# Prefix rows staged ahead, and the conv and merge stages of a hybrid retention block ordered by token blocks

## The reference

```python
mod = silu(c) @ w_ada + b_ada                     # six vectors of 1024 for each sequence
sh1, sc1, g1, sh2, sc2, g2 = split(mod)
u = rmsnorm(h) * (1 + sc1) + sh1
q, k, v, og, cb, cc, cx, ga, gb = split(u @ w_in) # 512, 512, then 1024 each
ret = groupnorm(retention(rotary(q), rotary(k), v))       # chunks of 64, carried state
y_ret = (silu(og) * ret) @ w_ret_out
y_conv = (cb * causal_conv3(cc * cx)) @ w_conv_out
h = h + g1 * ((sigmoid(ga) * y_ret + sigmoid(gb) * y_conv) @ w_o)
u2 = rmsnorm(h) * (1 + sc2) + sh2
h = h + g2 * (square(relu(u2 @ w_ff1)) @ w_ff2)
return rmsnorm(h)
```

## Time and profile before

| | us |
|---|---|
| median of 3 runs | 1334.42 (1331.57 to 1335.6) |
| the profiled execution | 1338.04 |
| its span, slowest core (core 2) | 1336.5 |
| spans of the eight cores | 1327.3 to 1336.5 |
| TensorE busy | 1231.7 |
| mean granted TensorE clock, share of full speed, by core | 0.966 to 0.974 |

### The profile page before, as it was taken

One profiled execution on the slowest core, in us unless ns is written; L12 is line 12 of the kernel. 1 busy time (PEld: TensorE's weight loads), 2 busy tenths in 40 slices (PEclk: granted clock), 3 DMA queues, 4 the chain that ended last, 5 costly groups with the idle time before them and its releaser, 6 DMA issues.

```text
span 1336.5 us, 18932 instructions; the slowest of 8 cores (1327.3 to 1336.5 us)
## 1 busy us (share of the span) xinstructions
PE 1231.7 (92%) x6288; PEld 582.0 (44%) x6288; DVE 489.3 (37%) x917; ACT 420.8 (31%) x714; POOL 488.4 (37%) x503
## 2 busy tenths in 40 slices
PE   2467799999999999998999999599999999999997
PEld 0233354444444455554444444254444444444443
DVE  5345366666312277776013234340000351000145
ACT  1354143222211167777321112243330023331011
POOL 1055310000000178886643361046660126663012
PEclk9688899999999999999999999799999999999999
DMA  9769170240713400000958819887545549954323
GB/s 169 181 159 210 50 96 1 38 58 1 91 28 41 69 11 1 1 2 8 144 91 128 151 19 243 200 206 105 80 67 92 95 157 155 139 86 70 65 87 126
DMA packets 86591, 124.33 MB, mean 93 GB/s; under 512 B 4704, under 2 KB 69216, under 8 KB 86496
## 3 DMA queue, kind: packets, MB, share of 16 engines
q0 software_dynamic: 67632, 70.26, 38.5%
q1 hardware_dynamic: 16560, 44.48, 10.5%
q10 hardware_dynamic: 2304, 8.39, 1.6%
HBM read 176.59 MB, written 16.78 MB: 145 GB/s over the span
## 4 chain that ended last, share of the span: by engine, by line
PE 85%; DMA 6%; DVE 3%; POOL 2%; issue 1%; another core or an unknown queue 1%; ACT 1%; DVEq 0%; POOLq 0%; SPq 0%; ACTq 0%
PE PS L304 83%; DMA ring<-w_ada 3%; DMA scr<-brow 2%; DMA h1s<-scr 2%; PE PS L450 1%; PE PS L934 1%; POOL Z L555 1%; DVE AR L896 1%; POOL rstd L433 0%; DVE scr L529 0%; DVE X L462 0%; POOL scr L535 0%; POOL scr L533 0%; DVE Y L437 0%
## 5 line engine op out<-in xcount | busy, mean ns | idle before, releaser
L304 PE MATMUL PS<-X,ring 128*128 128x512 bf16 x2560 | 567.9, 380 | 4.4 <-ACT scr L958 4.2
L304 PEld LDWEIGHTS PS<-X,ring 128*128 128x128 bf16 x2560 | 249.8, 98 | 303.9 <-issue 10.0
L304 PE MATMUL PS<-ring,Z 128*128 128x512 bf16 x896 | 213.2, 395 | 41.6 <-DVE G_t L422 15.6
L304 PEld LDWEIGHTS PS<-ring,Z 128*128 128x128 bf16 x896 | 89.1, 101 | 153.5 <-issue 59.6
L304 PE MATMUL PS<-Y,ring 128*128 128x512 bf16 x512 | 119.7, 381 | 2.0 <-DVE scr L765 2.0
L1134 ACT ACTIVATE scr<-PS 128x512 f32<-128x512 f32 x128 | 76.3, 597 | 140.7 <-PE PS L304 104.4
L304 PE MATMUL PS<-ring,X 128*128 128x512 bf16 x512 | 117.8, 379 | 2.4 <-DVE AR L896 2.4
L1153 DVE TENSOR_TENSOR AR<-PS,G_t 128x512 f32<-128x512 f32 x16 | 11.1, 691 | 295.0 <-PE PS L304 295.0
L304 PE MATMUL PS<-ring,Y 128*128 128x512 bf16 x512 | 113.4, 379 | 0.0
L757 ACT ACTIVATE scr<-PS 128x512 f32<-128x512 f32 x64 | 38.2, 597 | 189.4 <-PE PS L304 185.3
L236 POOL DMA_DIRECT2D ring<-w_in x17 | 16.6, 979 | 190.4 <-PE PS L304 190.4
(11 more groups left out here) (151 smaller groups left out, 1290.1 us busy)
## 6 DMA issues: line engine op xcount, KB each, us to landing
ring<-w_ff POOLq DMA_DIRECT2D x32, 1024.0 KB, 10.9
ring<-w_in POOLq DMA_DIRECT2D x17, 1024.0 KB, 16.6
scr<-x_main SPq DMA_DIRECT2D x32, 512.0 KB, 7.4
ring<-w_ada POOLq DMA_DIRECT2D x12, 1024.0 KB, 22.1
scr<-x_pre SPq DMA_DIRECT2D x16, 512.0 KB, 12.9
h1s<-scr SPq DMA_DIRECT2D x16, 512.0 KB, 7.4
scr<-h1s SPq DMA_DIRECT2D x32, 256.0 KB, 4.5
y<-scr ACTq DMA_DIRECT2D x16, 512.0 KB, 4.5
```

Source lines behind the costliest of these rows:

```text
L304: S.op("pe", lambda e: e.matmul(out, lhsT, rhs, start=start, stop=stop), reads=list(lkeys) + list(rkeys), writes=[okey])
```

## The change

It rearranges the order of the work, the buffers and the loads; the arithmetic of the reference is the same.

- Prefix rows: `load_x` picks its buffer by `x_stage`: tiles 6 to 13 go into X itself, which is empty then, later ones into scr buffers, G_t and the state tile. Pairs 3 to 7 of the prefix are issued together and wait for the key weights' chunk; the third pair waits for the fourth chunk. All prefix pairs come before the main ones. `x_norm` is split into `x_sq`, `x_rs` and `x_sc`, called in consecutive steps. The loop has 16 steps in place of 20. What followed it is reordered, with `p_m` for k = 4 and 5 ahead of and between the last tiles, and main block 0 transposed there; `mxs` puts normalised main rows in other places (X, then Z rows 4 to 7 and 0, 1).
- Conv stage: the first half runs token block by token block; main blocks 1, 2 and 3 are transposed behind groups 1 to 3, 5 to 7 and 9 to 11, two parts behind each third one; the last two pairs are normalised behind groups 4 and 6; the table follows from group 12 on, and six `mod_chunk` (g1, sc2, sh2) stand behind odd groups from 17 on.
- First merge: g2's two chunks.
- `mod_row` is gone, with its DMAs. `row_prep` builds diagonal blocks of the column vector in bfloat16 (high and low part) on DVE, and `row_mm` turns them into rows by 32 matmuls (16 a vector, of 128 columns with the all-ones tile) and copies them into G_t.
- Second merge: by token blocks, all four weight chunks resident, six banks. w_o is scaled behind groups 5 and 7. Ten of the output projection's sixteen steps (`O_step`) stand behind odd groups of blocks 1 to 3, six behind the merge.
- The MLP's hidden tiles take Z first, then Y.

```diff
                        wchunk(w_in, 0, 3072 + jg * 512)]
-        for jg in range(2):
-            chunks += [wchunk(w_co, 0, jg * 512), wchunk(w_in, 0, 7168 + jg * 512)]
+        for v in (2, 4, 3):
+            chunks += [ada(v, 0), ada(v, 1)]
+        chunks += [wchunk(w_co, 0, 0), wchunk(w_in, 0, 7168), ada(5, 0), ada(5, 1)]
...
         chunks += [wchunk(w_in, 0, 2048), wchunk(w_in, 0, 2560)]
-        chunks += [wchunk(w_ro, 0, 0), wchunk(w_in, 0, 6144)]
-        chunks += [ada(2, 0), ada(2, 1), ada(4, 0), ada(4, 1), ada(3, 0), ada(3, 1)]
-        chunks += [wchunk(w_ro, 0, 512), wchunk(w_in, 0, 6144 + 512)]
+        for jg in range(2):
+            chunks += [wchunk(w_ro, 0, jg * 512), wchunk(w_in, 0, 6144 + jg * 512)]
         chunks += [wchunk(w_o, 0, 0), wchunk(w_o, 0, 512)]
-        chunks += [ada(5, 0), ada(5, 1)]
         for mb in range(2):
...
         xbuf = {"n": 0}
 
+        x_extra = {24: "G", 25: 5, 26: 4, 27: 6, 28: "G", 29: 5, 30: "state", 31: 6}
+
+        def x_stage(i):
+            if 6 <= i < 14:
+                r = (i - 2) % 8
+                return X[:, r, :].bitcast(F32), XK("X", [r], range(4))
+            j = x_extra.get(i, (i if i < 6 else i - 14) % 6)
+            if j == "G":
+                return G_t[:, :], ["G", ("G", 1)]
+            if j == "state":
+                return state, ST4
+            return scr[j][:, :], SK(j)
...
+
+        def row_mm(diag, dk):
...
-                slot, skey = ring_use()
-                dma("sp", tmp, brow_d[:, g * 1024 + n * 512: g * 1024 + (n + 1) * 512], [], [tmpk], "bt")
-                b = mod_mm(slot, skey)
-                S.op("dve", lambda e, b=b, n=n: e.tensor_tensor(out=G_t[:, n * 512:(n + 1) * 512], in0=pa[b], in1=tmp, op=ALU.add),
-                     reads=[("pa", b), tmpk], writes=["G"])
+                b = nbank()
+                for kk in range(4):
+                    for a in range(2):
+                        mm(pa[b][:, kk * 128:(kk + 1) * 128], ("pa", b), ones_bf[:, :], ["ones"], dv[:, 2 * (n * 4 + kk) + a, :], [dk[n]],
+                           a == 0, a == 1)
+                S.op("act", lambda e, b=b, n=n: e.copy(out=G_t[:, n * 512:(n + 1) * 512], in_=pa[b]),
+                     reads=[("pa", b)], writes=["G", ("G", 1)])
...
+        pairs = [("p", t) for t in range(0, 16, 2)] + [("m", t) for t in range(0, 16, 2)]
         p_next = [0]
...
-            x_norm(kind, t)
-            pair_load()
+        def pair_do(stage):
+            kind, t = pairs[n_next[stage]]
+            n_next[stage] += 1
+            (x_sq, x_rs, x_sc)[stage](kind, t)
+            if stage == 2 and 6 <= n_next[2] < 10:
+                pair_load()
...
         pair_load()
         pair_load()
-        pair_load([("ring", 2)])
-        cload(predec[:, :], predec_d, "predec")
         for op_ in p_tab[0:10]:
             op_()
-        pair_norm()
+        pair_do(0)
+        pair_do(1)
         for op_ in p_tab[10:18]:
             op_()
+        pair_load([("ring", 3)])
+        cload(predec[:, :], predec_d, "predec")
         tmp_m = [rA[1], rB[1]]
         tmp_mk = [rAk[1], rBk[1]]
+        pair_do(2)
         mod_Tk(1, 0, [0, 1], tmp_m, tmp_mk)
         mod_gain(0, 0)
-        pair_norm()
+        pair_do(0)
+        pair_do(1)
+        pair_do(2)
         mod_Tk(0, 8, [2, 3], tmp_m, tmp_mk)
         s_wk, k_wk = ring_use()
+        for n in range(5):
+            pair_load([k_wk])
         for kp in range(4):
             p_tpart(0, kp, 4 + kp, "act" if kp % 2 == 0 else "dve")
-        pair_norm()
+        pair_do(0)
+        pair_do(1)
...
-        norm_at = {0, 1, 3, 4, 5, 6, 7, 8, 10, 12, 13}
-        for t in range(20):
+        sq_at = (0, 1, 3, 4, 5, 8, 9, 12, 13)
+        for t in range(16):
             g, i = t // 4, t % 4
-            if t < 16:
-                p_k(t)
+            p_k(t)
+            if n_next[2] < n_next[1]:
+                pair_do(2)
+            if n_next[1] < n_next[0]:
+                pair_do(1)
             if t >= 4:
                 p_m(t - 4, range(4), MA)
-            if g < 3 and i >= 2:
-                for kp in (2 * i - 4, 2 * i - 3):
-                    p_tpart(g + 1, kp, 2 + kp % 2, "act")
-            if g in (2, 3) and i < 2:
-                for kp in (2 * i, 2 * i + 1):
-                    m_tpart(g - 2, kp, 2 + kp % 2, "dve")
-            if t in norm_at:
-                pair_norm()
+            for kp in {2: (0, 1), 3: (2, 3), 5: (0,), 6: (1,), 7: (2, 3)}.get(t, ()):
+                p_tpart(1 if t < 4 else 2, kp, 2 + kp % 2, "act")
+            if g == 2:
+                p_tpart(3, i, 2, "act")
+            if t in sq_at:
+                pair_do(0)
+            if t in (13, 14):
+                pair_load()
...
-            if t in (2, 5, 8):
+            if t in (4, 7, 10):
                 ring_open(rstate["limit"] + 1)
...
+        for t in range(12):
+            p_m(t, [4], [2])
+        norm_tail()
+        p_m(12, range(4), MA)
+        m_tpart(0, 0, 1, "dve")
+        for t in range(12):
+            p_m(t, [5], [3])
+        norm_tail()
+        m_tpart(0, 1, 0, "act")
+        p_m(13, range(4), MA)
+        m_tpart(0, 2, 1, "dve")
+        for t in range(14, 16):
+            p_m(t, range(4), MA)
+        for k, b in ((4, 2), (5, 3)):
+            for t in range(12, 16):
+                p_m(t, [k], [b])
+        m_tpart(0, 3, 1, "act")
+        for t in range(16):
+            mm(pa[0], ("pa", 0), ones_bf[:, :], ["ones"], kd_ap[t], [kd_key[t]], t == 0, t == 15)
+        S.op("act", lambda e: e.copy(out=kbar, in_=pa[0]), reads=[("pa", 0)], writes=[SH(6, 0)])
+        for k in range(6):
+            m_evict(k, (MA + [2, 3])[k])
+        for k, b in ((6, 4), (7, 5)):
             for t in range(16):
-                p_m(t, [4 + k], [MB[k]])
-            m_evict(4 + k, MB[k])
-            if k < 2:
-                pair_norm()
+                p_m(t, [k], [b])
+            m_evict(k, b)
+        pair_load()
+        pair_load()
...
                 c_order = [(jj, tb) for jj in range(4) for tb in range(4)]
             for jj, tb in c_order:
                     j = jg * 4 + jj
...
-                        m_tpart(2 + n // 4, n % 4, nbank(), "act" if n % 2 == 0 else "dve")
-                    elif m_tab:
-                        m_tab.pop(0)()
-        assert not m_tab
+                    if n < 12:
+                        if n % 4 == 3:
+                            m_tpart(1 + n // 4, 2, nbank(), "act")
+                            m_tpart(1 + n // 4, 3, nbank(), "act")
+                        elif n % 4 > 0:
+                            m_tpart(1 + n // 4, n % 4 - 1, nbank(), "act")
+                        if n in (4, 6):
+                            norm_tail()
+                    elif n >= 17 and n % 2 == 1 and mod_list:
+                        mod_list.pop(0)[1]()
+                    else:
+                        for _ in range(3 if n < 14 else 2 if n < 17 else 1):
+                            if m_tab:
+                                m_tab.pop(0)()
+        assert not m_tab and not mod_list
...
-        phase_Y(Y, "Y", False)
+        def y1_hook(jg, jj):
+            if jg == 0 and jj < 2:
+                mod_chunk(5, 40, jj, G_t[:, 0:512], "G")
+
+        phase_Y(Y, "Y", False, y1_hook)
...
         o_slots = []
-
-        def y2_hook(jg, jj):
-            if jg == 0 and jj == 0:
-                mod_row(0, scr[2][:, 0:512], SH(2, 0))
-            elif jg == 0 and jj == 1:
-                mod_S(4, 16, 1, scr[2][:, 512:1024], SH(2, 1))
-            elif jg == 0 and jj == 2:
-                mod_T(3, 24, scr[2][:, 512:1024], SH(2, 1))
-            elif jg == 1 and jj == 1:
-                for n in range(2):
...
-        phase_Y(Y, "Y", True, y2_hook)
-        (s_o0, k_o0), (s_o1, k_o1) = o_slots
+        n_banks[0] = 6
+        bank_ctr[0] = 0
+        y2_ctr = [0]
+
+        def y2_group(tb, j):
+            jj = j % 4
+            by, bg = nbank(), nbank()
+            for (slot, skey), SRC, nm, b in ((s_ro[j // 4], Y, "Y", by), (s_ga[j // 4], X, "X", bg)):
+                for k in R8:
+                    mm(pa[b], ("pa", b), slot[:, k, jj * 128:(jj + 1) * 128], [skey],
+                       SRC[:, k, tb * 512:(tb + 1) * 512], [(nm, k, tb)], k == 0, k == 7)
...
+        def wo_scale(n):
+            o_slots.append(ring_use())
+            slot, skey = o_slots[n]
+            gb = G_t[:, n * 512:(n + 1) * 512].unsqueeze(1).to_broadcast([128, 4, 512])
+            for kh in range(2):
...
+            O_load(t)
+        o_next = [0]
+
+        def o_pop():
+            O_step(o_next[0])
+            o_next[0] += 1
+
+        for tb in range(4):
+            for j in range(8):
+                y2_group(tb, j)
+                if tb == 0:
+                    if j == 0:
+                        row_prep(32, scr[2][:, :], SK(2))
+                    elif j == 3:
+                        row_mm(scr[2][:, :], SK(2))
```

(14 more changed lines are left out.)

179 lines of the change are left out of this document (98 added, 81 removed).

## The result

The changed kernel takes **1315.9 us** (median of three executions, 1315.8 to 1319.8), the one before, beside it, 1333.6; ratio 0.9877, 95% interval 0.9848 to 0.9906. Faster, as forecast, but by 16 to 18 us and not by 49: 1285 was 31 us too low, and every execution lies outside the range of 1267 to 1310. The profiled execution took 1315.8 us, span 1314.3 on its slowest core (core 1); the other cores span 1299.8 to 1311.7.

The account below looks back on a forecast made before the run. TensorE's work and its 105 us of idle time, mostly in a DMA-bound head and the prefix loop, set the end. 1336.5 - 34.5 + 1.8 + 5 + 1.8 - 19.6 - 3.7 = 1287.3 us of span, 1285 us as median; range 1267 to 1310.

Parts of the forecast that it names:

- part 1: prefix rows staged: key weights land at 51.8 us, last kd at 118, conv stage at 138; head gains 34.5 us.
- The moved conditioning: 64 matmuls moved into the conv stage and first merge, where TensorE is full: sum 0, bound 8 us.
- The stall: output projection: TensorE waits for DVE, which waits for late brow rows; removing it gains 19.6 us with slow matmuls.
- The upper end of 133: prefix loop: the late bound for the last kd, 133 us, at 5.1 us a step, as now.
- rival B: prefix loop keeps 5.1 us a step, set by the engines' handshakes: gain 10.5 us, time 1309 us; chance 0.12.
- Part 2: conv stage's first half by token blocks: cost 5 us, bounds 0 and 14, with 1 us for two norm pairs.
- The boundaries: conv stage's first half: TensorE waits for ScalarE's evictions of X, 1.2 us lost each, 3.7 us at three block boundaries.
- Part 4: second merge and output projection: stall gone, 19.6 us; four-gate tail gone, 3.7 us; w_o scaling 0, at most 4 us.
- four-gate tail: second merge: 1.99 us of idle time and 1.7 of a slow pair behind it go with token blocks, 3.7 us.
- C: prefix loop: DMA slower for the ten tiles because of weight chunks, last rows 12 us later, 1297 us; chance 0.13.
- E: second merge: the second w_o tile or its scaling is late and DVE stands with it, 1299 us; chance 0.06.
- F: conv stage without slack: TensorE waits at each of 16 groups, 64 us in place of 5, 1344 us; chance 0.03.

Follow-up runs that it names:

- Experiment 6: four runs on the changed kernel's prefix loop: some scalings on ScalarE, transposes a step later, power earlier, waits filled with unread matmuls; whole times 1316.1 to 1327.5 us.
- experiment 1: the kernel before, with only g2's bias rows loaded ahead of the output projection's loads, into two buffers of their own: 1319.5 us, ratio 0.9891.
- experiment 4: the changed kernel with both halves of the second w_o chunk scaled on DVE: 1318.0 us in one execution; merge and projection 174.4 us, for 177.0.

## Why the prediction was right and wrong, step by step

**Right.** The key weights landed at 50.9 us (said 51.8): the DMA count of part 1 held. The moved conditioning cost what was said: the second half of the conv stage grew by the 10.4 us of its 48 matmuls. The output steps between the merge groups brought no wait but that for w_o, 2.5 us, and one of 0.3. The stall went, 15.6 us of waiting with the slow matmuls behind; the projection has no wait and clock 1.00. ScalarE loaded one table, 1.28 us, in merge and projection, as in the earlier trace rows, with Sigmoid, Square and Identity now alternating. The Trainium skill (ScalarE: Activation LUTs, Table sets: the hidden batching unit) has a load where a function lies outside the loaded set; by the trace none of these switches brought one.

**Part 1, the loop, 5.7 us short.** Two terms failed. The forecast followed the queues and had p10,11 scaled "about 79.5"; it was 81.2, and p_k(8) began at 90.6 and not at 88: 2.6 us. It charged the matmuls behind each wait at full clock, though the earlier trace rows show 24 at 7.35 and 8 at 3.41 us right behind a wait. That is 1.2 and 1.7 us at two places. Experiment 6 shows both and what they hang on: the power of the next pair queued behind a rotation and a decay. The other 3.1 us lie behind p_k(8): the forecast had 30 us from it to the last kd, and it took 33.1, because GpSimd's step there is 3.8 us and not the 3.3 that the durations of the kernel before gave. That the run with the earlier power ends at 119.0, near the forecast's 118, is luck: it starts p_k(8) at 83.3 us, 4.7 before the forecast, and takes 35.7 us from there, 5.7 more. The steps of 4.1 and "5.1 a step, as now" don't count the same thing: 4.1 runs to the last kd, 5.1 to the last key matmul. Counted to the last kd a step took 5.7 us before and 4.5 after; to the last key matmul, 5.1 and 4.0. The upper end of 133 and rival B rest on this mix.

**Part 1, behind the loop, 8.9 us short on the profiled core, 6.6 on the median one.** The text named the right chain: the bank of m_tpart(0,0), its eviction on DVE behind the scale of m8,9, "free at 121.5". It took the rows of m8,9 as present. They were not: issued at 112, landed at 126, in a stretch where the DMA engines were full. Rows earlier gave 3.8 us back. The other part, 22 us from kd to halo and not 20, are the waits for DVE at 122, 129 and 140 us; taking those away wasn't tried.

**Part 2, the conv stage, 2.7 us short.** The boundaries, said 3.7, cost 3.9: the working was right to 0.2 us. The norm pairs, charged at 1 us "for both", cost 3.7, of which 1.7 are the clock behind the wait. The reason given, DVE busy for 29.8 of 47.5 us and eight banks, speaks of shares; what decided was ScalarE's order, where two squares and the chain behind them stood ahead of four evictions.

**Part 4.** The w_o scaling, taken at 0 with 4 as its bound, cost 2.6, so the bound held and the value was wrong. Two other terms of the stage were off and nearly cancel. The stall was worth 21.7 us on the priced core, 2.1 more than said. The 3.7 us of the four-gate tail were hardly gained: the old order without the stall has 186.7 us (experiment 1), which is 174.7 with the 13.8 of moved conditioning off and the 1.8 of the row gates on, and the new one without the wait for w_o has 174.4 (experiment 4), with a wait of 1.77 us in place of the tail's 1.99. Together, 2.6 + 3.4 - 2.1 = 3.9, this is the stage's 3.8. "The queues passed over wait for nothing new" was false once: the new order of the projection's buffers put a store under the MLP's first Relu, 5.2 us on the profiled core. No part of the text asked who takes over the buffers of the last tiles.

**From span to median.** The text took 3.6 us off because the profiled execution was that much above the median, and took the whole stall of 19.6 us off as well. The stall is probably where that execution was long. Its median core spans 1334.0 us, that of the six comparable ones of the same kernel beside experiment 1 1328.1 to 1330.5 us; and in the stages that both kernels share, its median core differs little from the run without the stall (halo 173.1 and 171.6 us, from the end of the first half to the second merge 413.2 and 413.6). With one trace of each this is argued, not shown. With the 3.6 us, and 0.1 by which the median after lies above its profiled execution, the account closes: 27.1 + 3.6 + 0.1 = 30.8 of 30.9 us.

**The rivals.** None came alone. C's mechanism, rows late in full DMA engines, was there, at the main rows and not the prefix ones. E was there at a fifth of its price. F did not come near: the steps inside a block have no waits at all. The range failed because nearly all the misses had one sign, while the bounds were taken as not falling together, and because the arrival of the main rows and the buffer of the last tile had no bound at all.

## What to carry to other kernels

An idle stretch of TensorE can cost more than its length (here 2.0 us of waiting made 3.7 where the clock fell): take the matmuls behind every wait that is left at the length which the profile shows right behind a wait. A step price that was read where the bounding engine often stood idle is a lower end for a denser loop, as 3.3 us was for 3.8. When steps move, list for each queue what stands ahead of the one short instruction on which a long chain hangs (here a power of 0.7 us behind 2.7 us of rotation and decay), and for each buffer who writes it next. And a stall whose length differs by 8 us between cores is worth less in a typical execution than in a long one that was profiled, as 14.3 us were for 19.6.

## What the runs showed of the hardware

VectorE and GpSimd lengthened each other in the denser loop. GpSimd's rotation part in the rows of experiment 6 went from a constant 0.72 us to a mean of 0.88 (0.78 to 0.90 by group) with single ones of 0.99 and 1.10, its decay from 1.04 to a mean of 1.15 with single ones of 1.30; VectorE's scale of 128 x 1024 from a mean of 0.78 to 1.08. The Trainium skill (GPSIMD Engine Reference, Key points) says that GpSimd shares its SBUF interfaces with VectorE and that they contend when VectorE runs in a two-port mode or reads two SBUF inputs; the rows, in which both engines' instructions lengthen, agree with contention; which mode the scale runs in no row tells. Halving VectorE's share did not bring the end forward (experiment 6).

SyncE's own issue instruction, 0.33 us at 131 us, when the DMA engines had room (share 0.49 from 126 to 136), took 0.98 us at 112.44 and 1.2 us each for the three behind it, where they were full (0.99 from 112 to 126). The three small loads (decays and mask) ahead of them took SyncE from 107.24 to 112.40 us; so while the DMA engines are full, even small loads delay the rows behind them.
